# Diff attention: head norms and rotation inside the projection, staging by transfers, masks in spare rows

## The reference

```python
proj = h @ w_in                                     # q 1024, k 1024, v 1024, gate 1024 columns
q = _apply_rope(_rms_norm(q, q_g), cos, sin)        # q, k: (tokens, 8 heads, 2 maps, 64)
k = _apply_rope(_rms_norm(k, k_g), cos, sin)        # norm over the 64 features of one map
s = einsum('bhmqd,bhmkd->bhmqk', q, k) * scale      # query blocks of 128, keys up to the block's end
p = _chunk_causal_softmax(s, s0)                    # key chunk (64) <= query chunk (64)
wts = p[:, :, 0] - lam * p[:, :, 1]
o = _rms_norm(einsum('bhqk,bhkd->bhqd', wts, v), sub_g) * (1 - lambda_init)
x = x + (o * silu(gate)) @ w_out
```

## Time and profile before

| | us |
|---|---|
| median of 3 runs (4171.07 to 4177.68) | 4173.92 |
| profiled execution, its time | 4169.91 |
| profiled execution, span of the core | 4168.1 |
| first A: projection, norms and rotation, attention | 202.4, 72.2, 125.4 |
| second A: projection, norms and rotation, attention | 199.8, 73.2, 125.2 |
| attention of C | 99.2 |

### The profile page before, as it was taken

How to read it: one execution, slowest core, us unless ns; L and a number is a source line. 1 busy time by engine, 2 the same in 40 slices (tenths; PEclk the granted TensorE clock), 3 DMA queues, 4 the chain that set the end, 5 groups by cost and what they waited for, 6 DMA issues and landing times. The chain is left out here.

```text
span 4168.1 us, 44131 instructions
## 1 busy us (share of the span) xinstructions
PE 3579.3 (86%) x16764; PEld 2699.3 (65%) x16764; DVE 1801.7 (43%) x2767; ACT 1247.1 (30%) x2161; POOL 128.1 (3%) x120
## 2 busy tenths in 40 slices
PE   7977897887789776989778989789999987788998
PEld 5935664643669354458767865668888844546886
DVE  2256488324332565677352349632222214323333
ACT  3235333223422352257221222232121122424222
POOL 0011000001000110000000001100000000000000
PEclk9998899998999897999889999999999998999999
DMA  3200211200122002167211112111211010012231
GB/s 132 71 15 7 84 61 51 86 21 0 41 92 71 16 0 95 76 246 303 71 41 51 61 59 72 60 51 62 70 60 61 31 61 21 0 40 101 91 101 61
DMA packets 39969, 280.64 MB, mean 67 GB/s; under 512 B 4551, under 2 KB 4807, under 8 KB 8168
## 3 DMA queue, kind: packets, MB, share of 16 engines
q1 hardware_dynamic: 39848, 278.99, 18.7%
HBM read 264.30 MB, written 14.68 MB: 67 GB/s over the span
## 5 line engine op out<-in xcount | busy, mean ns | idle before, releaser
L398 PE MATMUL bank<-high,slot_high 128*128 128x512 f32 x3280 | 1200.4, 366 | 146.6 <-DVE low L327 102.6
L399 PE MATMUL bank<-low,slot_high 128*128 128x512 f32 x3280 | 1194.8, 364 | 0.0
L400 PE MATMUL bank<-high,slot_low 128*128 128x512 f32 x3280 | 1187.0, 362 | 0.0
L378 DVE TENSOR_TENSOR slot_low<-slot,slot_high 128x2048 fp32r<-128x2048 f32 (+1 forms) x162 | 366.8, 2265 | 1237.2 <-ACT slot_high L372 1237.0
L398 PEld LDWEIGHTS bank<-high,slot_high 128*128 128x128 f32 x3280 | 623.9, 190 | 265.9 <-issue 143.1
L372 ACT ACTIVATE slot_high<-slot 128x2048 fp32r<-128x2048 f32 (+1 forms) x162 | 306.6, 1893 | 1336.9 <-PE bank L400 1110.6
L400 PEld LDWEIGHTS bank<-high,slot_low 128*128 128x128 f32 x3280 | 622.1, 190 | 99.9
L399 PEld LDWEIGHTS bank<-low,slot_high 128*128 128x128 f32 x3280 | 624.2, 190 | 92.9 <-issue 1.9
L788 DVE TENSOR_REDUCE peak<-bank 128x1 f32<-128x128 f32 (+2 forms) x224 | 110.5, 508 | 254.2 <-PE bank L734 151.4
L845 ACT ACTIVATE prob<-bank,peak_bias 128x128 f32<-128x128 f32 (+2 forms) x224 | 119.8, 540 | 128.5 <-DVE peak_bias L796 127.9
L435 PE MATMUL bank<-slot_high,high 128*128 128x256 f32 x448 | 128.1, 286 | 27.3 <-DVE low L325 27.3
(11 more groups left out here) (328 smaller groups left out, 4483.5 us busy)
## 6 DMA issues: line engine op xcount, KB each, us to landing
mod_raw<-in_mod SPq DMA_DIRECT2D x48, 1024.0 KB, 5.1
slot<-in_gu SPq DMA_DIRECT2D x44, 1024.0 KB, 4.9
slot<-in_a_in SPq DMA_DIRECT2D x32, 1024.0 KB, 5.0
slot<-in_e_rest SPq DMA_DIRECT2D x16, 1024.0 KB, 4.9
slot<-in_down SPq DMA_DIRECT2D x16, 1024.0 KB, 4.9
spectra<-f_spectrum SPq DMA_DIRECT2D x12, 1024.0 KB, 3.9
h_spectrum<-spectra SPq DMA_DIRECT2D x12, 1024.0 KB, 5.1
slot<-in_a_out SPq DMA_DIRECT2D x8, 1024.0 KB, 5.5
```

Source lines behind the costliest of these rows:

```text
L378: dve.tensor_tensor(k.slot_low[s][:, 0:n], k.slot[s][:, 0:n], k.slot_high[s][:, 0:n].bitcast(F32), ALU.subtract).then_inc(k.low[s], 1)
L398: pe.matmul(out, wh, xh, start=kt == 0, stop=False)
L399: pe.matmul(out, wh, xl, start=False, stop=False)
L400: mm = pe.matmul(out, wl, xh, start=False, stop=kt == self.kt - 1)
```

## The change

Within the projection (`project_a`): the columns of the weights for query and key are reordered on the host, so that a slot's two result tiles hold the first and the last 32 features of four maps. The rotation then needs no permutation: DVE makes four products from the two tiles and adds or subtracts them. ACT squares both tiles out of the banks and copies them with the gain. DVE adds the two squares, so that one selection matmul per slot (the new L1043, plain f32) does for both. After four slots DVE and ACT make the reciprocal for them, split it in high and low parts, and two matmuls per slot (L1052 and L1053, one pass each) spread it into banks 4 and 5; DVE scales the tiles. The selection for slot n stands behind slot n+1 on PE, the spreading behind slot n+6. The projection's loops are written out. The tables are loaded by POOL's own DMA issues into the part of the gate tile that is not yet written.

`rotate_heads_a` is gone. In the attention of A the staging is done by DMAs that SP issues: eight per head, 32 rows of 512 tokens each, SBUF to SBUF, into q_now and k_now of each map. Rows 64 to 127 of these hold the mask, loaded once per stage by eight DMAs; the score matmul adds it, and L734 and its matmul are gone. In C the mask comes into the spare rows by three DMAs, L1640 and the mask matmul are gone, and POOL stages as before, with waits between heads.

```diff
-                        mm = pe.matmul(k.ps[b][:, n - 64:n], k.c("mask_row"),
-                                       k.c("mask_col", 64), start=False, stop=True)
-                    mm.then_inc(k.filled[b], 1)
+                    self.score(pe, hh, m, q, 0, n, k.ps[b], True).then_inc(k.filled[b], 1)
...
+    def sync(self, k, sp, u):
+
+        masked = k.named("masks_in")
+        for dst, src in self.masks:
+            sp.dma_start(dst, src).then_inc(masked.sem, 16)
+        if self.transfers:
+            self.stage_heads(k, sp, u)
...
+    def stage_heads(self, k, engine, u):
+        staged = [k.named(f"head_staged{hh}") for hh in range(2)]
+        b = self.s_banks(1)[-1]
+        for i in range(4):
             for hh in range(2):
+                if i:
+                    engine.wait_ge(k.filled[b], u.full(b, i * 4 + (2 * hh - 3)))
+                if self.transfers:
+                    for dst, src in self.stage(i, hh):
+                        engine.dma_start(dst, src).then_inc(staged[hh].sem, 16)
...
+        if self.masks:
+            pe.wait_ge(masked.sem, masked.at(16 * len(self.masks)))
         loop(pe, 4, turn)
...
-            rotate_heads_a(k, w, j, QK)
...
+            def select(n):
+                if n % 4 == 0:
+                    pe.wait_ge(k.drained[7], u[1].free(7, n // 4))
+                pe.wait_ge(paired.sem, paired.at(n + 1))
+                at = CON["four_rows"] + 12 - 4 * (n % 4)
+                mm = pe.matmul(k.ps[7][:, :], k.con[:, at:at + P], op.ring[2 * (n % 2)], start=n % 4 == 0,
+                               stop=n % 4 == 3)
+                mm.then_inc(k.filled[7] if n % 4 == 3 else added.sem, 1)
+
+            def widen(n):
+                b = 4 + n % 2
+                pe.wait_ge(k.drained[b], u[1].free(b, n // 2))
+                pe.wait_ge(inv_low.sem, inv_low.at(n // 4 + 1))
+                place = spread[:, (n % 4) * P:(n % 4 + 1) * P]
+                pe.matmul(k.ps[b][:, :], place, inv[0][:, :], start=True, stop=False)
+                pe.matmul(k.ps[b][:, :], place, inv[1][:, :], start=False, stop=True).then_inc(k.filled[b], 1)
+
+            def behind(slot):
+                if 1 <= slot <= 8:
+                    select(slot - 1)
+                if 6 <= slot <= 13:
+                    widen(slot - 6)
...
+                for t in range(2):
+                    act.wait_ge(k.filled[b + t], x.full(b + t, n // 2))
+                    act.activation(op.ring[2 * (n % 2) + t], k.ps[b + t][:, :], ACT.Square).then_inc(squared.sem, 1)
+                for t in range(2):
+                    act.activation(tile(2 * n + t), k.ps[b + t][:, :], ACT.Copy, scale=k.v(f"a_qk{j}", 2 * n + t))\
+                       .then_inc(k.drained[b + t], 1)
...
+                for dst, src, table in zip(part, (first, second, second, first), (cos, sin, cos, sin)):
+                    dve.tensor_tensor(dst, src, table, ALU.mult).then_inc(products.sem, 1)
...
+            def finish(slot, x):
+                if slot in (4, 8):
+                    average(slot // 4 - 1)
+                if slot < 8:
+                    pair_squares(slot)
+                    rotate(x, slot)
+                if slot in (4, 8):
+                    invert(slot // 4 - 1)
+                if slot in (5, 9):
+                    halve_inverse(slot // 4 - 1)
+                if 6 <= slot <= 13:
+                    scale(slot - 6)
```

More of the change, by code:

```diff
@@ L665, in __init__ @@
     def __init__(self, k, ctx, maps, keys, scale, stage, score, value, causal, out, neg_lam=None, ssq=None,
-                 order=(2, 1), clear=None):
-        self.order, self.clear = order, clear
+                 order=(2, 1), masks=(), halves=0, transfers=0):
+        self.order, self.masks, self.halves, self.transfers = order, masks, halves, transfers
+        self.staged_by = 16 * transfers if transfers else 1
         self.maps, self.keys, self.scale, self.stage, self.score = maps, keys, scale, stage, score
@@ L905, in stage @@
                     for m in range(2):
-                        ins = pool.tensor_scalar(k_now[hh][m][:, :], cols(QK, i * (2 * LAT) + (8 + hh) * LAT, LAT),
-                                                 k.c("map_rows", 1, m), None, ALU.mult)
-                    return ins
+                        rows = slice(64 * hh + 32 * m, 64 * hh + 32 * m + 32)
+                        for now, n in ((q_now, i), (k_now, 4 + i)):
+                            for half in range(2):
+                                at = (2 * n + half) * LAT
+                                yield now[hh][m][32 * half:32 * half + 32, :], QK[rows, at:at + LAT]
@@ L922, in attend, with _ @@
     with k.nc.Block() as block:
+        @block.sync
+        def _(sp):
+            att.sync(k, sp, u[0] if att.transfers else k.uses.copy())
         @block.gpsimd
         def _(pool):
-            att.pool(k, pool, u[0])
+            att.pool(k, pool, k.uses.copy() if att.transfers else u[0])
         @block.tensor
@@ L986, in project_a, with tile @@
         dot = k.sb("lam_dot", 4, ctx)
+        spread = k.sb("spread_exact", 4 * P, ctx, dt=F32R)
+        inv = [k.sb(f"head_rstd_{n}", LAT, ctx, dt=F32R) for n in ("high", "low")]
+        part = [G[:, x * LAT:(x + 1) * LAT] for x in range(4)]
+        cos, sin, spread_in = G[:, 4 * LAT:5 * LAT], G[:, 5 * LAT:6 * LAT], G[:, 6 * LAT:6 * LAT + 4 * P]
+        sums, rstd = k.root[:, 0:LAT], k.rstd[:, 0:LAT]
+        def tile(f):
+            return QK[:, f * LAT:(f + 1) * LAT]
         block = ctx.enter_context(k.nc.Block())
@@ new lines, in rotate @@
+            def rotate(x, n):
+                for t in range(2):
+                    b = qk.bank(n % 2, t)
+                    dve.wait_ge(k.drained[b], x.full(b, n // 2))
+                first, second = tile(2 * n), tile(2 * n + 1)
+                if n:
+                    dve.wait_ge(rotated.sem, rotated.at(2 * n))
+                for dst, src, table in zip(part, (first, second, second, first), (cos, sin, cos, sin)):
+                    dve.tensor_tensor(dst, src, table, ALU.mult).then_inc(products.sem, 1)
+                dve.wait_ge(products.sem, products.at(4 * n + 2))
+                dve.wait_ge(products.sem, products.at(4 * n + 4))
+                dve.tensor_tensor(first, part[0], part[1], ALU.subtract).then_inc(rotated.sem, 1)
+                dve.tensor_tensor(second, part[2], part[3], ALU.add).then_inc(rotated.sem, 1)
```

188 lines of the change are left out of this document (123 added, 65 removed).

## The result

The changed kernel takes 4034.56 us (median of 4 runs, 4029.29 to 4037.5) where the kernel before took 4175.8 on the same chip (4 runs, 4171.07 to 4183.06): a ratio of 0.9659, 95% interval 0.9641 to 0.9677. Faster, by 141 us; 148 were forecast. The profiled execution took 4035.5 us against 4169.91 before, 134.4 less.

The account below looks back on a forecast made before the run. PE alone was taken to bound the projection, with engines taking turns in norms and rotation. 155 - 20 - 22 - 1 + 24 + 5 + 7 = 148 us less gave 4022 profiled, 4026 as median, range 4006 to 4054.

Parts of the forecast that it names:

- gap removed: Between projection and first score in the two A stages: 77.0 + 78.0 = 155.0 us go.
- new start of the attention: Before A's first score: sixteen SP issues at 0.45 us and one landing, 10.1 us a stage, 20 in two.
- projection: Matmuls added on PE's path cost 10.9 us a stage, 22 in both; table loads at the start 1 in all.
- masks and POOL's silence, A: In A's attentions: dropped mask matmuls save 12 us a stage, 24 in both; undelayed DVE peak_bias 2.5, 5 in both.
- C: In the attention of C: first score 2.6 us sooner, 32 masks worth 4.5; together 7 us, bounds 1 and 9.
- rival (b): At A's attention start the sixteen transfers serialise: 41 instead of 10 us a stage, 4088 us; chance 0.08.
- cover argument: In the projection, added ACT and DVE work costs nothing: each cover holds with 1 to 2.4 us to spare.
- Rival (c): DVE or ACT becomes the bound in the projection: 24 us a stage, 4074 us; chance 0.07.
- rival (a): The attention gives nothing back, as waits grow and granted clock falls: 4060 us, half of that 4043; chance 0.15.
- Restaging: Within A's attention, SP's restaging of heads costs nothing: 6 us each, where PE first reads 18.4 us later.
- Rival (e): Slower than before because restaging in the attention comes late: at 33 us each, 4201 us; chance 0.02.
- (d): More gain: faster staging start, masks and DVE at their bounds, 4015 us; about 4000 if attention clock holds; chance 0.10.

Follow-up runs that it names:

- e5: Changed kernel with each staging transfer of A issued twice, the second time into spare tiles nobody reads: 4049.14 us, ratio 0.9700.
- e7: Changed kernel with each selection matmul in the projection done twice: 4056.45 us, ratio 0.9712.
- e3: Changed kernel without the rotation, DVE's four products and two combinations per slot left out: 4040.09 us, ratio 0.9686.
- e1: Changed kernel with the mask matmul put back after every score in all three causal attentions: 4057.89 us, ratio 0.9716.
- e6: Kernel before with the mask matmuls left out and no other part of the change: 4149.09 us, ratio 0.9942.
- e2: Changed kernel with POOL making its old staging copies in A's attentions, into spare tiles nobody reads: 4058.34 us, ratio 0.9725.
- after: The changed kernel itself, in its first set of runs and first profile: 4034.56 us, ratio 0.9659 to the kernel before.
- the nine profiles: Profiles of the changed kernel and follow-ups leaving the attention's PE, ACT, DVE, POOL instructions alone (one moves eight issues): attentions 106.9 and 109.6 us in the mean.
- e11: Changed kernel with POOL zeroing a spare tile, an instruction without input, at each staging of A's attentions: 4095.42 us, ratio 0.9799.
- e9: Changed kernel with the first head's four masks and eight staging transfers issued by SP within the projection: 4016.60 us, ratio 0.9610.
- e12: The changed kernel once more, unedited, in another set of runs: 4042.39 us, ratio 0.9674.
- e8: Changed kernel with the reciprocal of the first four slots taken before slot 4's combinations on DVE: 4041.29 us, ratio 0.9683.

## Why the prediction was right, step by step

| term | forecast | profile |
|---|---|---|
| gap removed | 155 | 155.0 |
| new start of the attention | -20 | -25.2 |
| projection | -23 | -24.0 |
| masks and POOL's silence, A | +29 | +29.3 |
| C | +7 | +3.8 |
| not touched by the change | 0 | -4.5 |
| sum | 148 | 134.4 |

**The gap** went whole, as the timeline said; nothing of the old chain is in the new one.

**The new start** was mis-sized. I took an issue at 0.45 us from loads and stores of whole tiles; these, of 32 and 64 rows, took 0.63. The landing, counted from the start of the last issue, was 2.3 instead of 2.5. It came to 12.6 us instead of 10.1, 5 us over two stages; e5 repeats the 0.63. The mechanism, issues in a row and one landing, held: rival (b) is out. Sixteen transfers in series at a fixed 2.0 us each would have been 32 us a stage, and e5's eight more would have cost 16, where they cost 5.06. The 2.0 us is the figure that the Trainium skill ("DMA: Bandwidth & Descriptors", section "Anatomy of one DMA") fits to transfers issued by GpSimd; on SP's queue here it was not paid for each transfer.

**PE's additions** of 10.9 us a stage and 1 at the start were 12.1 and 11.9. (A seam holds one matmul more behind slots 1 to 5, three behind 6 to 8 and two behind 9 to 13.) A selection was 0.85 to 0.95 (e7) against my 0.9; 0.9 us is the wait of the selection of slot 4. There my cover argument failed in a detail: I counted DVE's reciprocal, done by T(4) + 12.7, against the next halving and the first spreading, and overlooked that the selection behind slot 5 wants the same bank 7 that the reciprocal empties, at about T(4) + 11.8. As the prediction put it, it was paid once. Rival (c) is out by e3.

**Masks and POOL** came to 15.0 and 14.3 us a stage against 14.5, but by two errors in opposite directions, which cancelled. The masks were worth 7 to 11 a stage (e1: 7.8, 7.1; e6: 10.9, 7.4) and not 12. POOL's silence was worth 4 to 10 (e2: 6.9, 10.3; e6 against after: 4.0, 6.9) and not 2.5; for both stages that is 11 to 17 us (8 to 14 against the nine profiles' means) where my bound was 8. For the masks I saw the clock and the waits, and gave them 1 us of 13, where waits took up 3.4 of 11.2 in e1 and 4.5 of 15.5 in e6. So rival (a) is half a truth, for about a third of that term. For POOL I priced the delays as waits of PE (seven by my count, six by e11's memsets), and left out PE's own busy time at a lower clock: in e2 the waits grew by 0.4 us in all and the busy time by 6.5, and e11 shows both prices by themselves. That 29.3 met 29 is luck twice over, since with the nine profiles' means (106.9 and 109.6) in place of this one profile the term is 26.1. The parts are what to learn from.

**C**: the first score came 4.3 us after its barrier and not 3.4, before 6.1: 1.8 of the 2.6. The attention behind it is 93.2 - 88.6 = 4.6 shorter, against 4.5, and e1 and e6 (91.7, 88.3) confirm masks as its cause, where the kernels without them have 86.8 to 88.6. The two together are 6.4. The whole stage, from its first weight issue to the first issue of the output weights, shows only 3.8: its parts ahead of the attention took 2.6 us more (234.0 against 231.4), which nothing in the diff explains. In e2, whose edit doesn't touch C, they took 231.8, so this is no fixed cost of the change. The 4.5 us elsewhere are not explained either: 1.1 ahead of the first projection, 1.1 between the attention of C and the second projection, 2.1 behind the second A stage. That last part is 2541.8 us before and 2543.9 after, and 2541 to 2554 in the experiments' profiles.

**Restaging** cost nothing; e5 doubled it and it still cost nothing. Rival (e) is out. **(d)** as I wrote it needed a faster start; that was to be had, but only by moving the start (e9), not in this change.

The signs named for the profile: first score at 12.6, not 10 to 11; projection 12 longer, not 11. Past its first slots PE is busy 184.42 of 186.10 us at clock 1.00, as said; the 0.98 over the whole holds the start, as before. No DMA wait beyond the first, as said. The attention takes 118 us from its barrier and not 116.

What stays open: how much of the 7 to 10 us in e2 is POOL's doing and how much scatter of the clock, which differs by 0.01 and 0.07 between e12 and the first profile of the same kernel; and by what path POOL's short holds of DVE (0.4 us each) would lower it.

## What to carry to other kernels

When work moves under an engine that is never idle, what it adds on that engine is paid to the instruction, and what it adds elsewhere is free as long as every reader of a shared buffer, not only the next big one, gets it before it is due. Transfers ahead of a barrier's first consumer cost their issues, one after the other, so issue them in the stage before. Where TensorE waits often, price a delay by what it does to the clock as well (e11: 13.3 us of waits, 12.8 of longer busy time). Trust a term only when a kernel with that term alone has been run, and read its size from more than one profile: here two terms were off by some 3 to 6 us a stage, in opposite directions, and their sum by next to nothing.

## What was not expected of the hardware

An issue on SP took 0.61 to 0.64 us for 32 or 64 rows of 512 f32, where loads and stores of whole tiles took 0.45 to 0.56; on ACT's queue it was 0.63 to 0.65, and with two queues at once the first score came 3.4 us after the last issue ended, instead of 1.7.

A memset on POOL, with no input, held a DVE instruction of 128x2 elements for 2.83 us that otherwise takes 0.17. That the reciprocal behind it was held too (2.75 us) does not say whether by the same cause or by its place in the queue.

The same stretch with the same 368 records ran at different granted clocks in kernels whose edits leave the attention's matmuls alone: in the first stage from 0.98 (103.43 us, e3) to 0.89 (108.68 us, e8), in the second from 0.95 (106.92 us, after) to 0.86 (112.39 us, e5), some 5 us for 0.09 in each.
